# The order of the products in a split float32 matmul of an FFN's first projection

## What is computed

```python
def swiglu(x, w_in, w_out):
    gate, up = jnp.split(x @ w_in, 2, axis=-1)
    return (jax.nn.silu(gate) * up) @ w_out

def conv_glu(hn, w_in, conv_w, conv_b, w_out):
    u, gate_in = jnp.split(hn @ w_in, 2, axis=-1)
    c = (conv_w[0] * shift_right(gate_in, 2) + conv_w[1] * shift_right(gate_in, 1)
         + conv_w[2] * gate_in + conv_b)
    return (jax.nn.gelu(c, approximate=False) * u) @ w_out
```

## Time and profile before

| | |
|---|---|
| median of 3 runs | 1628.66 us (1626.01 to 1629.92) |
| span of the profiled execution | 1629.3 us |
| TensorE matmuls busy | 1497.1 us (92%), 8792 records |
| TensorE weight loads busy | 1284.3 us (79%), 8792 records |
| VectorE, ScalarE, GpSimd busy | 704.1, 550.6, 549.9 us |
| mean granted clock of TensorE | 0.951 |

### The profile page before, as it was taken

How to read it: one execution, slowest core, us unless ns; L and a number is a source line. 1 busy time by engine, 2 the same in 40 slices (tenths; PEclk the granted TensorE clock), 3 DMA queues, 4 the chain that set the end, 5 groups by cost and what they waited for, 6 DMA issues and landing times.

```text
span 1629.3 us, 21249 instructions
## 1 busy us (share of the span) xinstructions
PE 1497.1 (92%) x8792; PEld 1284.3 (79%) x8792; DVE 704.1 (43%) x885; ACT 550.6 (34%) x671; POOL 549.9 (34%) x209
## 2 busy tenths in 40 slices
PE   5999989999989999979979997999998888899996
PEld 4999978898668999668878855899967364899985
DVE  1545531353136454231564113566642171456654
ACT  3443310213124544321335111444342163444443
POOL 4655500031135554301021022546521044356541
PEclk9999989899999999989999768999999899999998
DMA  8555557332435555423400022455543402355540
GB/s 285 194 191 190 180 120 224 100 129 78 136 130 169 185 180 182 154 81 111 139 23 1 1 81 93 163 187 191 188 153 117 141 27 88 125 193 188 180 155 26
DMA packets 158212, 223.24 MB, mean 137 GB/s; under 512 B 5452, under 2 KB 135717, under 8 KB 158021
## 3 DMA queue, kind: packets, MB, share of 16 engines
q1 hardware_dynamic: 154284, 216.96, 40.4%
q10 hardware_dynamic: 3864, 5.38, 1.6%
HBM read 219.57 MB, written 2.62 MB: 136 GB/s over the span
## 4 chain that ended last, share of the span: by engine, by line
PE 85%; DVE 6%; ACT 4%; POOL 2%; issue 2%; DMA 0%; DVEq 0%; SPq 0%; POOLq 0%; ACTq 0%
PE ps L734 29%; PE ps L764 14%; PE ps L725 12%; PE ps L827 5%; PE ps L973 3%; PE ps L808 2%; PE ps L797 2%; PE ps L1098 1%; PE ps L958 1%; PE ps L1206 1%; PE ps L1222 1%; PE ps L890 1%; ACT weights_first_parts L1339 1%; PE ps L1093 1%; PE ps L1234 1%
## 5 line engine op out<-in xcount | busy, mean ns | idle before, releaser
L1689 POOL TENSOR_TENSOR weights_second_parts<-weight_bays,weights_first_parts 128x2048 fp32r<-128x2048 f32 x88 | 418.6, 4761 | 407.5 <-ACT weights_first_parts L1339 407.5
L1339 ACT ACTIVATE weights_first_parts<-weight_bays 128x2048 fp32r<-128x2048 f32 x132 | 249.8, 1909 | 174.9 <-PE ps L734 74.5
L734 PE MATMUL ps<-x_first_part,weights_first_parts 128*128 128x256 f32 x1408 | 199.0, 284 | 15.8 <-ACT x_first_part L1320 7.4
L725 PE MATMUL ps<-xT,weight_bays 128*128 128x256 f32 (+1 forms) x896 | 201.3, 386 | 2.6 <-DVE xT L1837 2.6
L734 PEld LDWEIGHTS ps<-x_first_part,weights_first_parts 128*128 128x128 f32 x1408 | 184.8, 192 | 21.2 <-issue 15.9
L734 PE MATMUL ps<-x_second_part,weights_first_parts 128*128 128x256 f32 x1408 | 201.3, 287 | 0.0
L734 PE MATMUL ps<-x_first_part,weights_second_parts 128*128 128x256 f32 x1408 | 198.5, 285 | 0.0
L725 PEld LDWEIGHTS ps<-xT,weight_bays 128*128 128x128 f32 (+1 forms) x896 | 171.5, 193 | 29.4 <-DVE xT L1837 3.3
L734 PEld LDWEIGHTS ps<-x_second_part,weights_first_parts 128*128 128x128 f32 x1408 | 184.9, 195 | 0.0
L734 PEld LDWEIGHTS ps<-x_first_part,weights_second_parts 128*128 128x128 f32 x1408 | 182.4, 193 | 0.0
L1863 DVE TENSOR_TENSOR hidden_second_part<-arena,hidden_first_part 128x512 fp32r<-128x512 f32 x44 | 117.9, 2679 | 42.4 <-ACT hidden_first_part L1329 42.4
(11 more groups left out here) (343 smaller groups left out, 1818.7 us busy)
## 6 DMA issues: line engine op xcount, KB each, us to landing
weight_bays<-in_w_ffn_in SPq DMA_DIRECT2D x44, 1024.0 KB, 5.1
weight_bays<-in_ffn_w_in SPq DMA_DIRECT2D x44, 1024.0 KB, 5.1
weight_bays<-in_w_ffn_out SPq DMA_DIRECT2D x22, 1024.0 KB, 4.9
weight_bays<-in_ffn_w_out SPq DMA_DIRECT2D x22, 1024.0 KB, 4.9
weight_bays<-in_w_in SPq DMA_DIRECT2D x19, 1024.0 KB, 5.4
weight_bays<-in_hyb_w_in SPq DMA_DIRECT2D x13, 1024.0 KB, 5.2
weight_bays<-in_ple_w_gate SPq DMA_DIRECT2D x8, 1024.0 KB, 4.9
weight_bays<-in_w_out SPq DMA_DIRECT2D x4, 1024.0 KB, 4.8
```

The source lines that it names most:

```text
L725: mm = nc.tensor.matmul(dst, lhs(k), xT[:, k] if rhs is None else rhs(k), start=(k == 0), stop=(k == n - 1), **kw)
L734: mm = nc.tensor.matmul(dst, w[:, k, j * P:(j + 1) * P], x[:, k], start=(n + k == 0), stop=(n == 2 and k == KD - 1))
L1339: nc.scalar.activation(hi, raw, ACT.Copy).then_inc(*w_hi_ready.inc(f, g, kind, of - g))
L1689: nc.gpsimd.tensor_tensor(lo, raw, hi, ALU.subtract).then_inc(*w_lo_g.inc(f, g, kind, of - g))
```

## The change

Inside `split_features` the 24 matmuls of a result stay the same and are put in another order. The products of the weights' second parts come first. Then, for each `k`, the first part of the weights is multiplied by `x_hi[:, k]` and directly after it by `x_lo[:, k]`. The wait for all of `x_lo` in the first result of an FFN now stands behind 8 matmuls instead of 16.

```diff
--- before.py
+++ after.py
@@ -727,11 +727,14 @@
 
             def split_features(dst, hi, lo, j, first=None):
 
-                for n, (w, x) in enumerate(((hi, x_hi), (lo, x_hi), (hi, x_lo))):
-                    if n == 2 and first:
-                        pe.wait_ge(*x_lo_d.at(first, 3))
-                    for k in range(KD):
-                        mm = nc.tensor.matmul(dst, w[:, k, j * P:(j + 1) * P], x[:, k], start=(n + k == 0), stop=(n == 2 and k == KD - 1))
+                for k in range(KD):
+                    nc.tensor.matmul(dst, lo[:, k, j * P:(j + 1) * P], x_hi[:, k], start=(k == 0), stop=False)
+                if first:
+                    pe.wait_ge(*x_lo_d.at(first, 3))
+                for k in range(KD):
+                    w = hi[:, k, j * P:(j + 1) * P]
+                    nc.tensor.matmul(dst, w, x_hi[:, k], start=False, stop=False)
+                    mm = nc.tensor.matmul(dst, w, x_lo[:, k], start=False, stop=(k == KD - 1))
                 return mm
 
             def ffn(f):
```

## The result

The changed kernel takes 1640.19 us in the median of six runs (1638.37 to 1644.71), and the kernel before 1629.29 (1625.97 to 1635.3). The ratio is 1.0071, with an interval of 1.0050 to 1.0091: it is slower by about 11 us. I had forecast 1631 us, no change that can be told. The profiled execution took 1638.91 us, with a span of 1637.2, which is 7.9 us above the span of the profile before. A run's time is 1.7 us more than its span, so the profile before belongs to an execution of about 1631.0 us. Among the executions of the kernel before that were timed beside the experiments one took 4101.61 us, and the ratios leave it out.

A forecast was written before the change was run, and what follows sets the result against it. The prediction took the FFNs to be bound by TensorE. It added 0 for steady results and 2.5 us for the FFN starts to 1629.3, giving 1631.8, or 1631.2 from the median; forecast 1631 us, range 1620 to 1640.

The forecast's parts named there:

- Steady results at 2.86 us: 176 results of 24 matmuls: reordering leaves each at 0.94 + 1.92 = 2.86 us, a change of 0.
- rival (a): Second matmul of each pair is cheaper with repeated weights: 14 us saved, 1617 us, at the extreme 1603; chance 0.17.
- rival (b): Alternating the moving tensor costs, over 2464 more changes: 1639 us at 3 ns each, at most 1680; chance 0.13.
- The standing: TensorE waits for x_lo after 8 matmuls at each FFN's start: 0.42 and three times 1.24, 4.1 us.
- first term: TensorE's wait for x_lo at the first FFN's start: 0.29 us plus hand-over, 0.42 us.
- other three: TensorE's waits for x_lo at the second to fourth FFN's starts: 1.24 us each with the hand-over.
- hand-over: Delay between one engine's end and TensorE's start, added to each wait for x_lo: 0.13 us.
- The clock: At the FFN starts, low clock returns at the same moment, so a microsecond standing costs 0.56 us; together 2.5 us.
- rival (c): Pause at an FFN's start keeps the clock low one more stretch, 1.5 us each: 1636 to 1637 us; chance 0.10.
- The sum.: Whole kernel: 1629.3 + 0 + 2.5 = 1631.8 us against the profiled execution, 1631.2 from the median.
- Nothing is given back: Wait for GpSimd at group 1's up moves with TensorE, so the 2.5 us reach the end.

The follow-up runs named there:

- early wait alone: Kernel before, old order in blocks of eight, with the wait for all of x_lo moved from behind 16 matmuls to behind 8: 1642.65 us, ratio 1.0072.
- work in the pause: Changed kernel plus four useless transposes ahead of the wait for x_lo in each FFN's first result: 1635.32 us, ratio 1.0044.
- the pairs alone: Changed kernel, but the first result of each FFN keeps the old order with its wait behind 16 matmuls: 1632.56 us, ratio 1.0023.
- the blocks: Kernel before with the second weights' product first, still in blocks of eight, wait behind 16 matmuls: 1630.92 us, ratio 1.0008.

## Why the prediction was wrong, by its steps

- **Steady results at 2.86 us, no gain and no cost of the pairs:** right. A result takes 2.86 us in the timeline after, with the loads all in place; rival (a), cheaper repeated weights, and rival (b), a costly alternation, are both out: the ninth to twenty-fourth matmul stand 120 ns apart as before. I had taken nothing for the first result of a group, and it costs 0.03 us, 1.2 us in all.
- **The standing:** right in place and near in size, but the equal totals are luck. The sum gave 0.42 and three times 1.24 us, 4.1 in all, and the idle time is 4.1. It was 1.01 to 1.03 us at each start, the first included: there the eight matmuls ran at the full clock (24.10 us on, a length of 1.18 us), as the low stretch came later than in the profile before. So the first term was too small and the other three too large. The two totals don't measure the same thing either. The sum counted from the moment at which the next matmul could have started, some 1.03 us behind the first, and from there to 469.79 it is 1.17 us at the second start. The hand-over that I took as 0.13 us was 0.06 there: VectorE ended `x_lo` at 469.73.
- **The clock, the step that failed.** I priced a microsecond of standing in the low stretch at 0.56 us with the words "If the clock comes back at the same moment as before". It did not: the low stretch was 6.6 us at the second to fourth start, where it had been 3.3, and at the first it lasted from 25.3 to 32.1 us, where in the profile before the matmuls at 213 ns had ended by 28.5 (their second block, from 26.04 us, is in the earlier trace rows). This is rival (c), which I had given 0.10, with the argument that the pause is short and matmuls fill the rest of the stretch. The early wait alone made the long stretch at the second to fourth start, and work in the pause put it back to 3.2 us there with the pause's length kept. So it is the standing without work that prolongs it. When it does so depends on where the stretch falls: at all four starts of the changed kernel the clock fell within 0.3 us of the pause's beginning (at 25.3, 469.0, 1011.8 and 1397.5 us), and at the first start of the early wait alone, where it was low already, the stretch didn't grow. With the longer stretch, the first two results of the four FFNs took 2.0, 2.5, 2.3 and 2.4 us more than before, 9.1 in all, where I had 2.5. Rival (c) at all four starts had 1637 us, so it had the mechanism and less than the size.
- **The sum.** In the profiled executions, 9.1 + 1.2 us, less 3.0: the kernel before had a low stretch behind group 1's wait in the third and fourth FFN (at 1028.6 and 1410.9 us), 1.5 us each, and the changed one does not. That makes 7.3 of the 7.9 us. Read directly, from the start of the first to that of the last result, the four FFNs take 7.1 us more. The rest lies outside them.
- **Nothing is given back:** right. The wait for GpSimd at group 1's `up` is 6.6 us in four times after the change as before. What came back is the 3.0 us of the two low stretches behind it, which this step had not considered.

Three smaller slips of the prediction don't touch this step. Without the hand-over its own prices give 0.16, twice 0.71 and 0.62 us, 2.2 and not 2.0. It put the span of 1629.3 us beside timed medians, though a time is 1.7 us more than its span. And it took the transposes of the earlier trace rows for two passes in a record: the rows show 110 ns for a record of 128 columns, and no run shows the number of passes.

The medians lie 11 us apart and not 7.9, as the two profiled executions were not median ones: the one before stood 1.7 us above its median and the one after 1.3 us below. Times follow the mean granted clock. In the kernel before, single runs go from 1625.6 us at 0.955 to 1638.4 at 0.944. At 0.947 to 0.948 the changed kernel takes 1638.4 to 1639.0 us, and the kernel before 1635.3 to 1635.5 at 0.947. By this some 3 us are there at an equal clock, and the rest of the 11 goes with a lower clock. The split is rough, since the mean can miss the first start's low stretch: the profile before counts its 4.1 us as full, which is 0.0013 of the mean, or some 1.5 us on this scale.

What stays open is why the pairs alone (1.0023) stand a little above the blocks (1.0008). The intervals overlap, and the steady results take the same time, so it may be no difference. Nor do the runs say why a block of second parts at a group's front costs 0.03 us, or what decides in a given execution whether a pause finds the clock about to fall.

## What to carry to other kernels

- A wait moved ahead on the engine that sets the end costs its standing, and on TensorE also what the clock does after it. Look at the granted clock around the place: here a pause of one microsecond that began as the clock fell doubled the low stretch.
- Putting matmuls with the same stationary tile next to each other gained nothing here, where each is issued with its own weight load and the load runs beside other matmuls. Count the loads before and after.
- Where TensorE waits some two microseconds for another engine, useless matmuls into a free place of PSUM can be worth more than they cost. Here 18 transposes made the kernel faster by 0.3%. The gain came in part from low stretches elsewhere that the trace no longer had.
- Spans of single profiled executions differ by a few microseconds from low stretches far from the change. Compare the changed stretch itself, here the first two results of an FFN, before reading anything from a span.

## What the runs showed of the hardware

- At these starts the clock stood at 0.50, the lower of its two levels, for about 3.3 us or for about 6.6. One more stretch of 3.3 us is 1.5 us in this stream. One program's runs spread over 8 to 13 us and get longer as their mean clock falls. That it is the number of such stretches that differs between them is likely, but only the profiled executions show the stretches.
- Transposes against the identity kept the clock at 1.00 through the 1.15 us of idle time behind them and into the FFN. In the kernel before, the clock also came back to 1.00 at 465.4 us, while TensorE had run transposes alone since 462.30. The Trainium skill has it in "TensorE: Matmul & The Clock Gate", section "Part 4: PE-mode transpose", that a transpose doesn't count as work for the clock in the way a matmul does (its figures there are for bf16). These two traces, with float32 transposes, don't agree, as far as they are of that mode, which the records (MATMUL) don't tell.
